# The output projection of a decoder block as seven quarter products instead of eight slabs

## The reference, cut to what matters

```python
mix = sigmoid(gate_a) * (oa @ w_up_hgrn) + sigmoid(gate_b) * (ob @ w_up_attn)   # [512, 1024]
x = x + mix @ w_o                                  # output projection, w_o is [1024, 1024]
hm = rms_norm(x, mlp_norm_g)
x = x + square(relu(hm @ w_mlp_in)) @ w_mlp_out    # D_FF = 4096
return rms_norm(x, final_norm_g)
```

## Time and profile before

| | |
|---|---|
| median of three executions | 730.28 us |
| profiled execution, own time | 729.67 us |
| its span in the profile | 727.9 us |
| PE (TensorE) busy | 709.9 us, 98% |
| DVE (VectorE) busy | 536.0 us, 74% |
| ACT (ScalarE) busy | 414.8 us, 57% |
| POOL (GpSimd) busy | 163.2 us, 22% |
| mean granted TensorE clock | 0.996 of full |
| DMA | 123.44 MB, mean 170 GB/s |

### The profile page before, as it was taken

One profiled execution on the slowest core, in us unless ns is written; L12 is line 12 of the kernel. 1 busy time (PEld: TensorE's weight loads), 2 busy tenths in 40 slices (PEclk: granted clock), 3 DMA queues, 4 the chain that ended last, 5 costly groups with the idle time before them and its releaser, 6 DMA issues.

```text
span 727.9 us, 11265 instructions
## 1 busy us (share of the span) xinstructions
PE 709.9 (98%) x4006; PEld 619.0 (85%) x4006; DVE 536.0 (74%) x820; ACT 414.8 (57%) x643; POOL 163.2 (22%) x203
## 2 busy tenths in 40 slices
PE   5999999999999999999999999999999999999995
PEld 4788878888888888888888889899898989898984
DVE  4676997767896754327644798888879797979894
ACT  6463554877853666544312675657575656666562
POOL 5421241112211446500000613202020211102012
PEclk9999999999999999999999999999999999999998
DMA  7456123544898554112621979999999999989432
GB/s 301 148 99 158 59 87 87 112 121 116 210 227 180 144 125 128 33 64 78 232 87 66 313 139 288 222 272 221 269 220 253 236 246 239 233 233 245 115 58 116
DMA packets 41838, 123.44 MB, mean 170 GB/s; under 512 B 3880, under 2 KB 6088, under 8 KB 41800
## 3 DMA queue, kind: packets, MB, share of 16 engines
q1 hardware_dynamic: 28256, 78.82, 31.9%
q0 software_dynamic: 10800, 39.33, 29.4%
q10 hardware_dynamic: 2744, 4.78, 3.0%
HBM read 79.92 MB, written 3.67 MB: 115 GB/s over the span
## 4 chain that ended last, share of the span: by engine, by line
PE 87%; DMA 4%; ACT 4%; DVE 2%; issue 2%; POOL 0%; POOLq 0%; ACTq 0%; DVEq 0%
PE bank L1820 11%; PE bank L1822 11%; PE bank L1821 11%; PE bank L1866 9%; PE bank L1870 8%; PE bank L1867 8%; PE bank L2110 6%; PE bank L2109 6%; PE bank L2107 6%; PE bank L2053 2%; PE bank L1828 2%; DMA s<-s 2%; PE bank L1961 2%; DMA br<-br 2%; PE bank L1837 1%
## 5 line engine op out<-in xcount | busy, mean ns | idle before, releaser
L832 ACT CAST whi<-raw 128x1024 fp32r<-128x1024 f32 x58 | 60.3, 1042 | 41.3 <-PE bank L1822 40.6
L1866 PE MATMUL bank<-hTh,whi 128*128 128x512 f32 x192 | 78.0, 406 | 1.0 <-DVE hTl L1278 1.0
L1820 PE MATMUL bank<-whi,ah 128*128 128x512 f32 x196 | 76.7, 392 | 0.4 <-DVE wlo L1597 0.4
L1821 PE MATMUL bank<-wlo,ah 128*128 128x512 f32 x196 | 76.4, 390 | 0.0
L1822 PE MATMUL bank<-whi,al 128*128 128x512 f32 x196 | 76.3, 389 | 0.0
L1870 PE MATMUL bank<-hTl,whi 128*128 128x512 f32 x192 | 75.1, 391 | 0.0
L1867 PE MATMUL bank<-hTh,wlo 128*128 128x512 f32 x192 | 74.9, 390 | 0.0
L2107 PE MATMUL bank<-hTh,whi 128*128 128x256 f32 x224 | 63.5, 283 | 0.0
L2110 PE MATMUL bank<-hTl,whi 128*128 128x256 f32 x224 | 63.4, 283 | 0.0
L2109 PE MATMUL bank<-hTh,wlo 128*128 128x256 f32 x224 | 63.4, 283 | 0.0
L1597 DVE TENSOR_TENSOR wlo<-br,whi 128x1024 fp32r<-128x1024 f32 x46 | 56.1, 1220 | 8.6 <-ACT whi L1072 8.6
(11 more groups left out here) (279 smaller groups left out, 1969.2 us busy)
## 6 DMA issues: line engine op xcount, KB each, us to landing
raw<-slabs SPq DMA_DIRECT2D x87, 512.0 KB, 4.4
br<-slabs SPq DMA_DIRECT2D x32, 512.0 KB, 5.0
wlo<-raw POOLq DMA_DIRECT2D x23, 512.0 KB, 5.1
s<-slabs SPq DMA_DIRECT2D x21, 512.0 KB, 4.4
br<-br POOLq DMA_DIRECT2D x21, 512.0 KB, 5.7
s<-s POOLq DMA_DIRECT2D x14, 512.0 KB, 7.0
raw<-raw POOLq DMA_DIRECT2D x7, 512.0 KB, 6.2
s<-raw POOLq DMA_DIRECT2D x7, 512.0 KB, 6.1
```

The source lines that it names most:

```text
L832: act.copy(whi[s][:, :], raw[s][:, :]).then_inc(hi_done, 1)
L1820: pe.matmul(dst, lh, rh, start=start, stop=False)
L1821: pe.matmul(dst, lh, rl, start=False, stop=False)
L1866: pe.matmul(dst, wh[:, k, c0:c0 + P], hi_[:, k, t0:T], start=k == 0, stop=False)
```

## The change

The 1024x1024 matrix and the mix are cut into quarters, 512x512 of the weights and 512 channels by 256 tokens of the mix, and the product is made of seven quarter products (Winograd's form of Strassen's scheme) instead of eight. Each takes two slots of the plan (14 slots in all, `NV` in place of `NPLAN`), a slot 12 matmuls of 512 columns.

- **Weights.** SP loads ten slabs for it, in the order x (which holds quarter 21), 22, 11, 12, y (21 once more), into memory that is free once the last gate product is done; SP waits for that, and before "12" also for the first sum. GpSimd issues four sums in place as accumulating DMAs, two of 512 KB each: x += 22, y += 11, x += 11, x += 12, the third after slot 3 has been split, the fourth after slot 7. `hi` and `lo` read these quarters instead of `raw`. The MLP's first four slabs are loaded after the last sum.
- **Mix.** VectorE makes four sums of mix quarters (`mix_sum`), ScalarE casts them (`mix_hi`), VectorE subtracts (`mix_lo`), all 128x1024.
- **Results.** Products 3 and 4 accumulate onto the banks of product 0 (and 3), product 6 onto those of product 1. VectorE adds to y 16 times (`y_add`) instead of 8, from banks read more than once.
- **Order.** Product 5 ends tokens 0 to 255, product 6 the left columns of tokens 256 to 511. TensorE transposes token tiles 0 and 1 (`turn_y`, six banks each) in the last slot before its last six matmuls, tiles 2 and 3 after them, then two banks whole.
- **Store.** ScalarE itself issues the store of its half of the last tile.

The diff, cut to its core (what is left out declares semaphores and replaces `NPLAN` by `NV` and `PLAN` by `plan`):

```diff
@@ -136,6 +136,13 @@
+        wq = {k: [place(f"wq{k}{c}", at_[c], SLAB) for c in range(2)]
+              for k, at_ in (("11", (48, 52)), ("22", (56, 60)), ("x", (64, 68)), ("12", (72, 76)), ("y", (80.5, 199.5)))}
+        WO_FORM = ("11", "x", "12", "x", "y", "22", "x")
+        WO_SLAB = {"11": 0, "12": 2, "x": 4, "y": 4, "22": 6}
+        wm = [place(f"wm{i}", 169 + 4 * i, SLAB) for i in range(3)]
+        wsh = [place(f"wsh{i}", at_, SLAB, F32R) for i, at_ in enumerate((145, 104, 113, 117))]
+        wsl = [place(f"wsl{i}", at_, SLAB, F32R) for i, at_ in enumerate((149, 108, 121, 125))]
         y = place("y", 153, NT * D)
...
@@ -346,11 +360,13 @@
+        LO_PART[n_wo] = 0
+        LO_PART[n_wo + 7] = LO_PART[n_wo + 13] = None
...
@@ -368,23 +384,37 @@
+        WO_BANKS = ((4, 5), (6, 7), (0, 1), (4, 5), (4, 5), (2, 3), (6, 7))
...
-        MLP_K = [4, 0, 5, 6, 7, 1, 2, 3]
+        MLP_K = [4, 0, 5, 1, 2, 3, 6, 7]
...
@@ -394,6 +424,17 @@
+        def source(n):
+            if not n_wo <= n < NV:
+                return raw[n % SLOTS], (raw_in[n % SLOTS], raw_loads(n))
+            p, c = (n - n_wo) // 2, (n - n_wo) % 2
+            return wq[WO_FORM[p]][c], (wq_in[WO_FORM[p]] if p in (0, 2, 5) else ws_in[p], 32)
...
@@ -520,6 +561,14 @@
+        wo_h = [mix_part(mxh3, 0, 0), four(wsh[0]), mix_part(mxh3, 1, 0), four(wsh[1]), four(wsh[2]), four(wsh[3]), mix_part(mxh3, 1, 1)]
...
@@ -623,11 +672,21 @@
-            for n in range(SLOTS, NPLAN):
+            for n in range(SLOTS, n_wo):
                 load(n)
+            b, u = tiles[n_gb + 7][0]
+            sp.wait_ge(full[b], u + 1)
+            for k in ("x", "22", "11", "12", "y"):
+                if k == "12":
+                    sp.wait_ge(ws_in[1], 32)
+                for c in range(2):
+                    sp.dma_start(wq[k][c][:, :], slabs[n_wo + WO_SLAB[k] + c]).then_inc(wq_in[k], 16)
+            sp.wait_ge(ws_in[6], 32)
             for m in range(4):
-                load(NPLAN + m)
-            b, u = tiles[n_wo + 7][-1]
+                n = NV + m
+                sp.wait_ge(*split_done(max(v for v in range(n_wo) if v % SLOTS == n % SLOTS)))
+                sp.dma_start(raw[n % SLOTS][:, :], slabs[NPLAN + m]).then_inc(raw_in[n % SLOTS], 16)
+            b, u = wo_tile(6, 1)
...
@@ -645,8 +704,6 @@
-            sp.wait_ge(S["act_fin"], 1)
-            sp.dma_start(out_t[NT - 1][:, 0:512], ys3[:, NT - 1, 0:512]).then_inc(out_done, 16)
...
@@ -753,10 +810,25 @@
+            def wo_sum(to, of, signal):
+                for c in range(2):
+                    pool.dma_start(wq[to][c][:, :], wq[of][c][:, :], accum_op=ALU.add).then_inc(signal, 16)
+            pool.wait_ge(wq_in["x"], 32)
+            pool.wait_ge(wq_in["22"], 32)
+            wo_sum("x", "22", ws_in[1])
+            pool.wait_ge(wq_in["11"], 32)
+            pool.wait_ge(wq_in["y"], 32)
+            wo_sum("y", "11", ws_in[4])
+            pool.wait_ge(*split_done(n_wo + 3))
+            wo_sum("x", "11", ws_in[3])
+            pool.wait_ge(wq_in["12"], 32)
+            pool.wait_ge(*split_done(n_wo + 7))
+            wo_sum("x", "12", ws_in[6])
...
@@ -1049,11 +1122,26 @@
+            def mix_hi(i, of, scale=1.0):
+                act.wait_ge(S["wm_done"], i + 1)
+                act.activation(wsh[i][:, :], of[:, :], ACT.Copy, scale=scale).then_inc(S["wsh_done"], 1)
+            def wo_mix(n, p):
+                if (n, p) == (n_wo - 2, 2):
+                    mix_hi(0, wm[0])
+                if (n, p) == (n_wo, 3):
+                    mix_hi(1, wm[1], -1.0)
+                if (n, p) == (n_wo + 1, 2):
+                    mix_hi(2, wm[2])
+                if (n, p) == (n_wo + 1, 3):
+                    mix_hi(3, wm[0])
...
@@ -1240,6 +1328,8 @@
+            act.wait_ge(S["act_fin"], 1)
+            act.dma_start(out_t[NT - 1][:, 0:512], ys3[:, NT - 1, 0:512]).then_inc(out_done, 16)
...
@@ -1342,16 +1433,80 @@
+            def y_add(p, q, r_, c, sign, after):
+                wait_full(wo_tile(p, q))
+                yy = y3[:, 2 * r_ + q, 512 * c:512 * c + 512]
+                if after:
+                    dve.wait_ge(S["wy_done"], after)
+                return dve.scalar_tensor_tensor(out=yy, in0=bank[wo_tile(p, q)[0]][:, :], scalar=0.5 * sign, in1=yy,
+                                                op0=ALU.mult, op1=ALU.add)
+            def wo_evict(v, p):
+                q = p // 2
+                if p % 2 == 0:
+                    return
+                if v == 3:
+                    dve.wait_ge(y_in, 16)
+                    y_add(0, q, 0, 0, 1.0, 0).then_inc(free[WO_BANKS[0][q]], 1)
+                if v == 8:
+                    y_add(1, q, 1, 1, -1.0, 0).then_inc(free[WO_BANKS[1][q]], 1)
+                if v == 6:
+                    dve.wait_ge(free[WO_BANKS[0][q]], wo_tile(0, q)[1] + 1)
+                    y_add(2, q, 0, 0, 1.0, 0).then_inc(free[WO_BANKS[2][q]], 1)
+                if v == 7:
+                    y_add(3, q, 1, 0, 1.0, 0).then_inc(free[WO_BANKS[3][q]], 1)
+                    if q:
+                        lo(n_wo + 7 + AHEAD)
+                if v == 9:
+                    dve.wait_ge(free[WO_BANKS[1][q]], wo_tile(1, q)[1] + 1)
+                    y_add(4, q, 1, 1, -1.0, 0).then_inc(S["wy_done"], 1)
+                    y_add(4, q, 0, 1, -1.0, 0).then_inc(free[WO_BANKS[4][q]], 1)
+                if v == 11:
+                    dve.wait_ge(free[WO_BANKS[4][q]], wo_tile(4, q)[1] + 1)
+                    y_add(5, q, 0, 1, -1.0, 0).then_inc(free[WO_BANKS[5][q]], 1)
+                if v == 13:
+                    dve.wait_ge(free[WO_BANKS[3][q]], wo_tile(3, q)[1] + 1)
+                    dve.wait_ge(S["wy_done"], 2)
+                    y_add(6, q, 1, 0, 1.0, 0).then_inc(free[WO_BANKS[6][q]], 1)
+                    if q:
+                        lo(n_wo + 13 + AHEAD)
+            def mix_sum(i, to, a_, b_, op):
+                dve.tensor_tensor(four(to), a_, b_, op).then_inc(S["wm_done"], 1)
+            def mix_lo(i, of, sign=1.0):
+                dve.wait_ge(S["wsh_done"], i + 1)
+                dve.scalar_tensor_tensor(out=wsl[i][:, :], in0=of[:, :], scalar=sign, in1=wsh[i][:, :].bitcast(F32),
+                                         op0=ALU.mult, op1=ALU.subtract).then_inc(S["wsl_done"], 1)
+            def wo_mix(n, p):
+                v = n - n_wo
+                if (v, p) == (-2, 0):
+                    dve.wait_ge(S["mix_done"], 4)
+                    mix_sum(0, wm[0], mix_part(tha3, 0, 0), mix_part(tha3, 0, 1), ALU.subtract)
+                if (v, p) == (-1, 0):
+                    mix_lo(0, wm[0])
+                if (v, p) == (0, 0):
+                    dve.wait_ge(S["mix_done"], 8)
+                    dve.wait_ge(S["wm_done"], 1)
+                    mix_sum(1, wm[1], four(wm[0]), mix_part(tha3, 1, 1), ALU.add)
+                if (v, p) == (0, 1):
+                    mix_sum(2, wm[2], mix_part(tha3, 1, 1), mix_part(tha3, 0, 1), ALU.subtract)
+                if (v, p) == (1, 0):
+                    dve.wait_ge(S["wm_done"], 2)
+                    dve.wait_ge(S["wsl_done"], 1)
+                    mix_sum(3, wm[0], four(wm[1]), mix_part(tha3, 1, 0), ALU.subtract)
+                if (v, p) == (2, 0):
+                    mix_lo(1, wm[1], -1.0)
+                if (v, p) == (3, 0):
+                    mix_lo(2, wm[2])
+                if (v, p) == (4, 0):
+                    mix_lo(3, wm[0])
...
@@ -1871,8 +2027,22 @@
+            def wo_part(p, q, k, wh, wl):
+                bu = wo_tile(p, q)
+                if k == 0:
+                    wait_free(bu)
+                dst, cols = bank[bu[0]][:, :], slice(q * P, (q + 1) * P)
+                onto = p in (3, 4, 6)
+                pe.matmul(dst, wo_h[p][:, k, cols], wh[:, k % 2, :], start=k == 0 and not onto, stop=False, skip_group_check=True)
+                pe.matmul(dst, wo_h[p][:, k, cols], wl[:, k % 2, :], start=False, stop=False, skip_group_check=True)
+                ins = pe.matmul(dst, wo_l[p][:, k, cols], wh[:, k % 2, :], start=False, stop=k == 3, skip_group_check=True)
+                if k == 3:
+                    ins.then_inc(full[bu[0]], 1)
+                return ins
...
@@ -1906,9 +2076,11 @@
-                    if j < 4 and p == 0:
-                        pe.wait_ge(S["mxl_done"], 2 * j + 2)
-                    ins = token_part(n, p, mxh3, mxl3, tiles[n], 2 * (j % 4), j % 4 == 0, j % 4 == 3)
+                    if p == 0 and j in (0, 4):
+                        pe.wait_ge(S["mxl_done"], 4 + j)
+                    if p == 0 and j in (2, 6, 8, 10):
+                        pe.wait_ge(S["wsl_done"], {2: 1, 6: 2, 8: 3, 10: 4}[j])
+                    ins = wo_part(j // 2, p // 2, 2 * (j % 2) + p % 2, slab_view(whi, s, 2), slab_view(wlo, s, 2))
...
@@ -2059,24 +2231,30 @@
-            for n in range(NPLAN):
-                for p in range(PARTS):
-                    mms(n, p)
-                    for s in woven[n][p]:
```

(51 more changed lines are left out.)

69 lines of the change are left out of this document (45 added, 24 removed).

## The result

The changed kernel takes 735.28 us (median of four executions, 734.92 to 735.80), beside 729.84 (729.29 to 730.54) for the kernel before in the same session: a ratio of 1.0077, 95% interval 1.0065 to 1.0090. It is slower by some 5.4 us, and the time lies above the predicted range. The profiled execution took 734.92 us, of which 733.2 are span, at a mean clock of 0.993.

A forecast was written before the change was run, and what follows sets the result against it. TensorE, busy 98% of the span, was taken as the bound. Terms -5.44 + 0.67 + 2.2 + 2.5 + 1.4 + 0 = +1.3 us gave 731.0 for the profiled execution, carried to 731.6 for the median; range 727.9 to 734.3.

The forecast's parts named there:

- The matmuls: TensorE in the projection: 168 matmuls instead of 192, at the same 0.2267 us distance, 5.44 us less.
- the handover: From the projection's last matmul to the MLP: 12 transposes ahead of the last six matmuls, +0.67 us.
- The sum x += 11: Slot 6 waits as this sum shares the DMA engines with y's load: stall 2.3 us, 0.2 at slot 7; bounds 0 and 5.
- rival D: A stall so long that the clock falls; half-clock matmuls cost 2 us more, with the later sum 735; chance 0.05.
- The price of a sum: An accumulating DMA of 512 KB lands after 5.2 us when alone, its work taken as 2.6 us of all DMA engines.
- Slot 4: TensorE waits for VectorE's subtraction: 0.6 us from VectorE alone, 1.6 from the late quarter 11, stall 2.2.
- Slot 8: Product 4 waits for VectorE's addition of product 3: stall 1.4 us, bounds 1.0 and 1.6.
- The store: At the kernel's end, ScalarE issuing its half of the last tile gains 0 us, bounds -0.35 and +0.1.
- B: Slower: the sum x += 11 is ready later still, at 372.3, costing 1.9 us more, so 733.5; chance 0.25.
- C: Cheaper sums: accumulating transfers take a plain load's 3.4 us, giving -1.3, so 729.0; chance 0.08.
- A: The transfers hide: only VectorE's 0.6, 0.3 and 1.4 us of waits remain, -2.5, so 727.8; chance 0.22.

The follow-up runs named there:

- the rearranged kernels: Changed kernel with quarter 11 and y loaded earlier and x += 11 replaced by a second copy z: 726.45 us; with VectorE's sums and product 2's addition later, late transposes: 723.59.
- the cut kernel with later sums: Changed kernel without the load of y, x += 11 cut to 128 columns, VectorE's mix sums and last two subtractions moved to later slots: 726.62 us, ratio 0.9960.

## Why the prediction was wrong, point by point

**The matmuls** were right, and **the handover** nearly. 168 matmuls, 0.2267 us apart where the clock is full and nothing waits (351.81 to 362.46 is 47 distances), -5.44. The handover is 0.82 for 0.67: the 12 transposes cost 1.35 for 1.39, and the first copy of `hTh` starts 1.42 us after the last slot (403.11) where I had 1.2.

**The term that failed is "The sum x += 11"**, 2.5 us where 6.59 + 2.44 = 9.0 came. Its mechanism was the right one: slot 6 waits for VectorE's subtraction, this for ScalarE's cast, this for the pair, and the pair shares the DMA engines with the load of y. Taking either away ended the wait. What was wrong is the count of work. I had two pieces of work, the load and the pair, 5.2 us each, from 360.1 on, which gave 370.4. But SP's loads of "12" and y wait for the first sum and were issued at 345.37 and 346.22, so that y (the weights' quarter) came late and GpSimd issued y += 11 only at 354.48; my working had no time for this pair at all. With it there are three of 5.2 us: 354.48 + 2.1 + 15.6 = 372.2, and 373.76 was measured. The same count misses by 1.5 in two more executions, those of the late transposes (355.01 gives 372.7, cast at 374.26) and of both stores by SP (355.37 gives 373.1, cast at 374.61). These 1.5 to 1.6 us no run explains, and no run takes y += 11 away and leaves the other two, so its part is counted, not shown by an experiment; that the load and x += 11 hold each other up is shown. From there the step runs as written: cast and subtraction 2.3 us (2.4 predicted), the subtraction ready 3.3 us later than I had it, and slot 6 due at 369.53 instead of 370.4 since slot 4 waited less: 2.4 + 3.3 + 0.9 = 6.6. The other 2.44 is the half clock behind the wait, which the sum had at nothing and left to rival D; the "some 4 us of matmuls" at half clock that D is priced by stand in no row of the kernel before, and 5.0 us were measured (376.12 to 381.1).

**The price of a sum was right only for a sum alone.** The 5.2 us of the earlier trace rows are a single transfer's. A pair's median was 5.6 in the run without the load of y (4.6 for the first, 6.6 for the second, which is the same 2.5 us of work each), 6.8 for y += 11 beside the load's start, and 12.6 for x += 11 beside most of it. By the Trainium skill, "SBUF — State Buffer", section "The DMA setup-cost knee", the estimate for 512 KB would be 2 us and 1.2, 3.2; every accumulating row of this size is above it, the busiest four times as long.

**Slot 4** waited 1.32 for 2.2. The cast came at 340.19, as predicted (340.6); of its lateness VectorE made up more by the last slab of `ub` than I allowed it, starting slot 4's subtraction at 362.63. That subtraction stood behind three sums, and either remedy, the earlier quarter or the later sums, removed the whole wait. I had added the two causes, 0.6 and 1.6, as if each had its own time.

**Slot 8** didn't wait, since VectorE caught up while TensorE waited at slot 6 and worked at half clock. Where slot 6 doesn't wait, slot 8 does: 1.10 to 1.14 in four of the runs, for 1.4 predicted, and 1.75 in that with the later sums.

**The store** was right, 0: the last byte comes 3.0 us behind the last operations by either issuer. The longer end, +0.58, wasn't in the sum.

**The rivals.** B (the sum later still) and D (the clock falls) both came true, and the text had their sum, 735, beside which 735.3 was measured. That it meets so well is luck: B priced the sum by the slowest single transfer seen, not by a third piece of work, and the two make 6.4 us of the step that cost 9.0; slots 4 and 8, with 2.3 less than in the sum, and the MLP, with 1.0 less, made up for it. The fault was the chance: 0.25 and 0.05, as if D were a thing apart. The clock had nothing left to decide once the wait was several us long: the bound of 5 us of wait, which gives 731.6 + 5 - 2.3 = 734.3, should have carried D's 2 us with it, so that the range reached 736.3. C, cheap sums, is refuted: even without the load of y the pair needed 7.2 us. A, the transfers hide, is what the rearranged kernels did; of the 2.3 us of VectorE that I had left in it, 1.10 remained at slot 8, and nothing once the sums and product 2's addition stood later.

**The balance.** Stage +5.82; from the MLP's first matmul to the last of all 724.36 - 405.34 = 319.02 instead of 320.03, -1.01, of which 0.4 is one wait for `wlo` that the changed kernel's execution didn't have. The rest no run explains: it is 319.53 in the kernel before with the unused semaphores, and 318.63 to 319.73 in the eleven variants of the changed kernel, so it may be in part an effect of the change; the end +0.58; the start of the stage -0.10. Together +5.3, the difference of the spans.

## What to carry to other kernels

Before loads are placed, list every transfer that is in flight in the same stretch, those of the change itself too, with its issue time and its share of the DMA engines, those that accumulate in memory at twice a plain load's work (here 2.5 us for 512 KB beside 1.3): two that are harmless alone cost 9 us of TensorE's time together. A source that is made by accumulation should not wait for its target to be read: here one more copy in memory (z) took the longest chain away. In an engine's own program, put what another engine needs next ahead of what is needed in ten slots; here VectorE had time for 21 us of new work, and only its order cost something.

## What the runs showed of the hardware

**A long wait is paid twice.** TensorE had nothing to do from 369.53 (its last matmul started at 369.30). The clock was still full from 373 to 374 and 0.65 in the us after; it then stayed at half, 1.2 GHz, until 381, although matmuls ran from 376.12:

```profile
373.00:374.00 1.00, 0.00 (x0) 0.00 (x0) 0.00 (x0) 0.24 (x1) 0.00 (x0) 1.00 0.04 4
374.00:375.00 1.00, 0.00 (x0) 0.00 (x0) 0.16 (x1) 1.00 (x2) 0.00 (x0) 0.65 0.00 0
```

Matmuls were then 0.427 us apart instead of 0.227, and the wait of 6.59 cost 9.03. Waits of up to 1.75 us (the cut kernel with later sums) left the clock at 1.00.

**Accumulating transfers and a plain load slow each other.** The load of 2 MB took 15.5 us beside the two pairs, and 7.9 where they were out of its way. Which of them pays depends on the order of issue. With quarter 11 first, the load was issued 3.0 us before the first pair and took 8.6 us, as if alone, while the pairs took 9.0 and 12.9. In the changed kernel it was issued 2.0 us behind the first pair, and that pair took 6.8 and the load 15.5. The end of the whole was the same, a cast at 374.03 or 373.76.
